# Splitting the softmax normalization of a sliding-window attention between VectorE and ScalarE

## What is computed

```python
scores = jnp.where(mask, q @ k_band * (HEAD_DIM ** -0.5), -jnp.inf)
m = jnp.maximum(jnp.max(scores, axis=-1, keepdims=True), sink)
p = jnp.exp(scores - m)
denom = jnp.sum(p, axis=-1, keepdims=True) + jnp.exp(sink - m)
p = (p / denom)
o = p @ v_band
y = o * jax.nn.silu(g)
return y @ w_out
```

## Time and profile before

| | us |
|---|---|
| median of 3 runs | 2513.62 |
| lowest, highest | 2511.29, 2516.64 |
| profiled execution, its own time | 2515.32 |
| profiled execution, its span | 2513.5 |
| TensorE busy in the span | 2316.5 (92%) |
| VectorE busy | 1581.0 (63%) |
| ScalarE busy | 1149.6 (46%) |
| GpSimd busy | 1190.1 (47%) |

### The profile page before, as it was taken

The page is one execution under the profiler, slowest core; times in us unless marked ns, Lnnn a source line. Parts: engine busy times, 40 slices in busy tenths (PEclk is TensorE's granted clock), DMA queues, the critical chain, the costliest instruction groups (busy, mean ns, idle before and its releaser), DMA issues. The chain is left out here.

```text
span 2513.5 us, 44927 instructions
## 1 busy us (share of the span) xinstructions
PE 2316.5 (92%) x15008; PEld 2116.4 (84%) x15008; DVE 1581.0 (63%) x3039; ACT 1149.6 (46%) x1707; POOL 1190.1 (47%) x491
## 2 busy tenths in 40 slices
PE   5898868998899999999999977889999999999997
PEld 4896858886899999997888867789999999788886
DVE  2475766255199766646777754318976665677776
ACT  4334434443344567753333333435447776333332
POOL 5878706847578866661000014357886666200000
PEclk9999999999999999999999988999999999999999
DMA  6445405534545544445565553144554444555554
GB/s 222 164 142 173 151 18 164 180 101 153 164 151 171 174 141 142 134 164 180 193 193 194 193 169 118 58 161 158 169 175 143 140 135 159 183 193 193 194 194 136
DMA packets 109272, 398.29 MB, mean 158 GB/s; under 512 B 12688, under 2 KB 13072, under 8 KB 108432
## 3 DMA queue, kind: packets, MB, share of 16 engines
q1 hardware_dynamic: 104240, 379.63, 45.9%
q10 hardware_dynamic: 4960, 17.69, 2.1%
HBM read 394.13 MB, written 3.15 MB: 158 GB/s over the span
## 5 line engine op out<-in xcount | busy, mean ns | idle before, releaser
L1604 POOL TENSOR_TENSOR w_lo<-ring,w_hi 128x1024 fp32r<-128x1024 f32 x474 | 1183.0, 2519 | 960.4 <-ACT w_hi L810 959.5
L810 ACT ACTIVATE w_hi<-ring 128x1024 fp32r<-128x1024 f32 x722 | 743.1, 1056 | 633.4 <-PE X L416 427.3
L414 PE MATMUL G<-hT_hi,w_hi 128*128 128x256 f32 x2880 | 827.7, 287 | 32.7 <-POOL w_lo L1604 12.0
L415 PE MATMUL G<-hT_lo,w_hi 128*128 128x256 f32 x2880 | 818.4, 284 | 0.0
L416 PE MATMUL G<-hT_hi,w_lo 128*128 128x256 f32 x2880 | 818.2, 284 | 0.0
L414 PEld LDWEIGHTS G<-hT_hi,w_hi 128*128 128x128 f32 x2880 | 556.1, 193 | 37.8 <-issue 17.5
L415 PEld LDWEIGHTS G<-hT_lo,w_hi 128*128 128x128 f32 x2880 | 556.7, 193 | 0.3 <-issue 0.2
L416 PEld LDWEIGHTS G<-hT_hi,w_lo 128*128 128x128 f32 x2880 | 556.0, 193 | 0.0
L414 PE MATMUL X<-w_hi,hT_hi 128*128 128x512 f32 x1024 | 400.5, 391 | 8.9 <-DVE hT_lo L1509 8.9
L415 PE MATMUL X<-w_lo,hT_hi 128*128 128x512 f32 x1024 | 400.1, 391 | 0.0
L416 PE MATMUL X<-w_hi,hT_lo 128*128 128x512 f32 x1024 | 399.8, 390 | 0.0
(11 more groups left out here) (253 smaller groups left out, 2365.1 us busy)
## 6 DMA issues: line engine op xcount, KB each, us to landing
ring<-slabs_in SPq DMA_DIRECT2D x722, 512.0 KB, 3.8
big<-rows_in ACTq DMA_DIRECT2D x10, 512.0 KB, 5.9
big<-rows_in ACTq DMA_DIRECT2D x3, 1024.0 KB, 15.7
big<-keys_in ACTq DMA_DIRECT2D x2, 1024.0 KB, 6.4
h_kept<-h ACTq DMA_DIRECT2D x2, 1024.0 KB, 8.6
h<-h_kept ACTq DMA_DIRECT2D x2, 1024.0 KB, 4.9
h<-x_in ACTq DMA_DIRECT2D x1, 1024.0 KB, 8.3
big<-ws_in ACTq DMA_DIRECT2D x1, 1024.0 KB, 23.0
```

The source lines that it names most:

```text
L414: nc.tensor.matmul(out, a_hi, b_hi, start=start, stop=False, skip_group_check=True)
L415: nc.tensor.matmul(out, a_hi, b_lo, start=False, stop=False, skip_group_check=True)
L810: nc.scalar.activation(w_hi[:, 2 * j + half, :], ring[j][:, half * 1024:(half + 1) * 1024], ACT.Copy).then_inc(hi_ready, 1)
L1604: Q.tensor_tensor(w_lo[:, 2 * j + half, :], ring[j][:, half * 1024:(half + 1) * 1024], w_hi[:, 2 * j + half, :], ALU.subtract).then_inc(sp ...
```

## The change

In the first attention alone (`sinks` is true only there), VectorE multiplies only the first half of a unit's heads by the reciprocal sums: two of four in units 0 to 3, one of two in units 4 to 11. ScalarE multiplies the other half, with an activation `Copy` whose scale is the head's column of `rden`. The reciprocal signals a new semaphore `rden_b`, on which ScalarE and VectorE both wait; ScalarE's last multiplication counts up `p2_b`, and TensorE waits for `p_b` and `p2_b` before each transpose. ScalarE's new piece `normalize_half` for unit k stands in its list ahead of the exponentials of unit k+2 and, for units 10 and 11, ahead of the copy of the unit's transposes.

```diff
--- before.py
+++ after.py
@@ -499,6 +499,8 @@
                     stage = f"{name}_{kind}{k}"
                     if kind == "t":
                         pe.wait_ge(sem(f"p_{name}"), k + 1)
+                        if name == "b":
+                            pe.wait_ge(sem(f"p2_{name}"), k + 1)
                     if kind == "v":
                         first = PV_AFTER[name][k - 1] + 1 if k else 0
                         for u in range(first, PV_AFTER[name][k] + 1):
@@ -885,8 +887,21 @@
                                              ACT.Copy).then_inc(free, 1)
 
             def attention(name, sinks, from_psum=None, round_to=None):
+                def normalize_half(k):
+
+                    s, row = units[name][k]
+                    n = s.shape[1]
+                    act.wait_ge(sem(f"rden_{name}"), k + 1)
+                    for u in range(n // 2, n):
+                        last = nc.scalar.activation(s[:, u, :], s[:, u, :], ACT.Copy, scale=rden[:, row + u:row + u + 1])
+                    last.then_inc(sem(f"p2_{name}"), 1)
+
                 for kind, k in attention_order(name):
                     stage = f"{name}_{kind}{k}"
+                    if sinks and kind == "s" and k >= 2:
+                        normalize_half(k - 2)
+                    if sinks and kind == "t" and k >= UNITS[name] - 2:
+                        normalize_half(k)
                     if kind == "s":
 
                         s, row = units[name][k]
@@ -1186,8 +1201,12 @@
                         link(V.tensor_tensor(rsum[:, m], rsum[:, m], esink[:, m], ALU.add))
                     else:
                         x_read(dve, f"{name}_s{k}")
-                    link(V.reciprocal(rden[:, m], rsum[:, m]))
-                    for u in range(s.shape[1]):
+                    if sinks:
+                        V.reciprocal(rden[:, m], rsum[:, m]).then_inc(sem(f"rden_{name}"), 1)
+                        dve.wait_ge(sem(f"rden_{name}"), k + 1)
+                    else:
+                        link(V.reciprocal(rden[:, m], rsum[:, m]))
+                    for u in range(s.shape[1] // 2 if sinks else s.shape[1]):
                         last = V.tensor_scalar(s[:, u, :], s[:, u, :], rden[:, row + u:row + u + 1], None, ALU.mult)
                     last.then_inc(sem(f"p_{name}"), 1)
```

## The result

The changed kernel takes 2523.19 us (median of 9 runs, 2519.29 to 2528.89) against 2513.49 us of the kernel before (9 runs, 2511.29 to 2516.64). The ratio is 1.004 with a 95% interval of 1.0029 to 1.0052, so the change makes the kernel some 10 us slower. I had forecast +3.65 us and no measurable change. The sign of the sum was right and its size was not; the measured time lies just inside the range, which went to 2523.5.

A forecast was written before the change was run, and what follows sets the result against it. VectorE was taken to set the attention's pace between value products. Delays of 0.85 + 0.45 + 0.6 + 1.75 gave +3.65 us: 2519.0 on the profiled execution, 2517.3 against the median; range 2511.5 to 2523.5.

The forecast's parts named there:

- What bounds the attention: First attention: VectorE sets the pace between two value products; halving its multiplications takes at most 3.7 us off.
- The prices: ScalarE's piece: 0.68 us for two heads, 0.49 for one of 256 columns; VectorE saves 0.40 or 0.265 per unit.
- The order of ScalarE's list as the mechanism: Exponentials of unit k+2 and a copy precede ScalarE's piece, so the transposes wait for them; its load doesn't decide.
- The sum in four pieces: Delays to the starts of value products v0, v1, v2 and v3: +0.85, +0.45, +0.6 and +1.75, together +3.65 us.
- TensorE's own durations in the sum: Ahead of value products: four transposes taken at 0.49 us, scores at 1.03; low clock counted only in the last piece.
- rival B: TensorE's clock falls inside the attention: +6.6 us at 2520.2, or +12 at 2525.8 if low through v2; chance 0.17.
- Its first case: Clock falls before v0: t1 and s4 cost 1.35 us more, v0's matmuls 1.8; stated total +6.6, at 2520.2.
- The gap before t0: TensorE's idle time before unit 0's transposes grows from 3.39 to 4.3 us, perhaps enough to make its clock fall.
- My sign of being wrong: In the new profile, a granted TensorE clock below 1 before 355 us would show the forecast wrong.
- Rival A: VectorE keeps the pace and the saving comes through: at most -3.7 us, 2509.9; chance 0.13.
- Rival C: Hand-offs between engines cost 0.15 instead of 0.05 us at some 20 places: +2 on top, 2519.3 to 2519.6; chance 0.10.
- The rule of the Trainium skill: Multiplications belong on VectorE, not ScalarE: by that rule alone, 5.5 us added against 3.7 removed loses 1.8 us.

The follow-up runs named there:

- left_out: Changed kernel without ScalarE's half and without TensorE's wait for it, so the output differs: 2515.65 us against 2514.59, ratio 1.0004.
- load_only: Against the kernel before: VectorE multiplies all heads, ScalarE does the added work on a scratch tile, TensorE doesn't wait for it: 2514.26 us against 2514.59, ratio 1.0000.
- wait_only: Against the kernel before: VectorE multiplies all heads, TensorE waits for a one-column ScalarE activation where the half stood: 2520.61 us, ratio 1.0018.
- early: Changed kernel with ScalarE's piece one unit earlier in its list, ahead of the exponentials of unit k+1: 2515.1 us, ratio 1.0012.
- filled kernels: Kernel before and changed kernel, both with unread matmuls filling TensorE's idle time in the attention: 2513.04 us (ratio 0.9999) and 2516.85 us (ratio 1.0009).
- keep_after: Changed kernel with TensorE's idle time in the attention filled by matmuls whose result is never read: 2516.85 us, ratio 1.0009.
- before_again: The kernel before, no edit, run once more for another trace: stage 56.45 us.
- after_third: The changed kernel, no edit, run again for a third trace: stage 64.76 us.
- after_again: The changed kernel, no edit, run once more for a second trace: median 2522.78 us against 2514.04, ratio 1.0042.
- keep_before: Kernel before with TensorE's idle time in the attention filled by matmuls whose result is never read: 2513.04 us against 2514.04, ratio 0.9999.
- tail_only: The change at units 10 and 11 alone, against the kernel before: 2518.26 us, ratio 1.0013.

## Why the prediction was wrong, step by step

- **What bounds the attention: right.** VectorE set the pace; left_out gets most of the removed list time back up to v3.
- **The prices: right.** 0.68 and 0.49 us for ScalarE's pieces, 0.40 of VectorE's list for two of four heads.
- **The order of ScalarE's list as the mechanism: right and shown.** Of the stage's loss, load_only without the wait has 0.2 us, wait_only without the load has all, and early with both has a third to a half.
- **The sum in four pieces: right for a clock that holds.** The filled kernels differ by 1.17, 0.39, 0.58 and 1.27 us up to v0, v1, v2 and v3, in all 3.4, where I had 0.85, 0.45, 0.6 and 1.75, of which 0.45 was the low clock that the filling removes: 3.2. Some 0.4 of the 1.17 comes from the one stretch of low clock in keep_after; without it some 3.0 would be left.
- **The failed step: TensorE's own durations in the sum.** I took transposes at 0.49 and scores at 1.03 us and left the value products at their lengths, from a trace whose clock held until 358 us. The low clock I kept out of the sum up to v2, as rival B with a chance of 0.17. Measured against my four pieces, the three traces of the changed kernel need 2.44 to 2.78, 0.81 to 2.08, 0.57 to 1.83 and 1.63 to 1.64 us. Together that is 6.7 to 7.1 where I had 3.65. The 3.1 to 3.4 us between them have two parts. One is a value product at low clock, v1 in the first trace (3.20 us) and v0 in the two others (3.62) where keep_after has 1.95: 1.25 to 1.67 us. The products stood on the chain before as well. The other, 1.7 to 1.8 us, is about what the slow steps add that the new wait puts on the chain: 0.4 for the transposes of unit 0 (1.08 us), 0.9 for the scores of unit 3 behind them (1.91) and 0.4 for the transposes ahead of the slow product (1.08 or 1.09). In before_again and load_only, steps as slow as these cost 0.3 and 0.1 us. After_third lost another 1.5 in v3, where the clock recovered later.
- **Rival B: right in its price, wrong in its reason.** Its first case, a fall before v0, is what after_again and after_third show. Its own terms, 1.35 and 1.8, add up to 3.15 and not to the 2.9 that it states; measured are 3.4. In the first trace the fall came back at v1, a case that it didn't have, and the near sum of 3.1 is luck. The gap before t0 that was to cause the fall didn't grow to 4.3 us: it was 3.06 to 3.17 in the changed kernel, 4.09 in wait_only and 3.40 in load_only, and in all of these the transposes of unit 0 took 1.08 to 1.12 us; in the kernel before they took 0.66 behind the same 3.39. The clock had fallen once already in the first scores, ahead of everything that the change touches (4.54 instead of 2.92 us); keep_before had the same, and its v0 came only 0.13 later for it; in the changed kernel t0 came 7.6 to 7.7 us after the start of such scores, in keep_after, whose scores took 2.92, 7.4. What makes the clock fall at one place and not at another stays open. My sign of being wrong, a granted clock below 1 before 355 us, came true, but two of the three traces of the kernel before show it as well (340 to 350 us), so it told nothing of the change.
- **Rival A: wrong**, as left_out shows: not even the saving alone can be told in the time. **Rival C: wrong.** The filled kernels leave 0.2 us for them (3.4 against 3.2), and the transposes start 0.09 to 0.11 us after ScalarE's piece where I took 0.05, not 0.15.
- **The rule of the Trainium skill**, page ScalarE: Activation LUTs, section Rules for kernel authors (multiplications on VectorE, not ScalarE): its direction holds here, but no run shows the price per element to be the cause; load_only, with all of that work, loses 0.2 us in the stage and nothing that can be told in time.
- **From the stage to the time.** The stage gives +7.2 us on average and the second attention +0.5 to +0.8 (below), the medians +9.7 and +8.7. The rest of 1 to 2 us stays open. The spread of the times tells nothing here: the changed kernel's runs differ by 9.6 and 14.9 us, those of the kernel before by 5.4 in the first comparison and by 10 to 16 in the later, longer ones.

## What to carry to other kernels

When a piece of work moves to an idle engine, read the place it takes in that engine's list, not the engine's load: here the added work cost 0.2 us of the stage, and waiting for it at that place brought all 7. Ask, too, which engines' steps a new wait puts on the chain, and price them at the durations that they have at their worst, not at those of one good trace. TensorE's low clock cost 0.1 to 0.3 us on transposes and scores while VectorE set the pace. With TensorE waiting for ScalarE it cost 3.1 to 3.4 us up to v3, over half of it on such steps and the rest in a value product.

## What was not expected of the hardware

The second attention, whose code the change doesn't touch, takes longer in the changed kernel. VectorE's wait for ScalarE's rounding there, before and after:

```profile
DVE M_oTl L1569 <- ACT M_oTh L910: 13.3, 4, 5.3
```

```profile
DVE M_oTl L1588 <- ACT M_oTh L925: 14.1, 4, 5.8
```

The three traces of the kernel before have 13.3 to 13.4 us there, those of the changed one 13.9 to 14.1; left_out has 14.1, load_only 13.8, wait_only 13.3 and tail_only 13.4. In one of these waits ScalarE ended at 1594.41 and VectorE went on at 1594.51 in the kernel before; in the changed one the two are 1602.99 and 1603.46. It goes with the program, not with the execution, and neither the wait nor the added ScalarE work sets it; the cause was not found.

Work that nobody reads can hold the clock, though not surely: with 0.7 us of filling in each round, keep_before's granted clock was 1.00 from 320 us to the last product, and v3 fell from 5.43 to 3.81 us, while keep_after had 0.58 from 324 to 328. The stage won 2.0 us of it. In the time of the whole kernel that can't be seen.
